# Doubling levels on half the columns, masks for four heads at once, and another place for GpSimd's selections

## What is computed

```python
# delta rule, per head and chunk: decay is exp of a difference of running sums, beta a gate
a = jnp.where(strict, jnp.einsum('nbhid,nbhjd->nbhij', k_beta, k) * decay, 0.0)
t_inv = lax.linalg.triangular_solve(a + eye, jnp.broadcast_to(eye, a.shape),
                                    left_side=True, lower=True, unit_diagonal=True)
u = t_inv @ (v * beta[..., None])
...
# choice of experts: 8 heads, the 16 best pairs out of 128 x 128 keys
sc = jnp.einsum("thpk,hpnk->thpn", q, sub_keys).astype(jnp.float32)
s_top, i_top = lax.top_k(sc, PEER_TOPK)
cand = s_top[:, :, 0, :, None] + s_top[:, :, 1, None, :]
cand_idx = i_top[:, :, 0, :, None] * PEER_NKEYS + i_top[:, :, 1, None, :]
best, pos = lax.top_k(cand.reshape(n_tok, PEER_HEADS, kk), PEER_TOPK)
idx = jnp.take_along_axis(cand_idx.reshape(n_tok, PEER_HEADS, kk), pos, axis=-1)
...
act = jax.nn.gelu(jnp.einsum("phkd,pd->phk", u_tab[idx], t))   # by experts, then summed with v_tab[idx]
```

## Time and profile before

| | |
|---|---|
| median of three runs | 2365.32 us |
| the profiled execution | 2366.43 us |
| its span on the core | 2364.6 us |
| mean granted TensorE clock | 0.958 of full speed |
| delta stage, first instruction to last | about 299.6 to 407 us of the span |
| choice of experts, the part with the 16 early tiles | about 1050 to 1179 us |
| TensorE busy | 91% of the span |
| GpSimd busy | 32% |

### The profile page before, as it was taken

One profiled execution on the slowest core, in us unless ns is written; L12 is line 12 of the kernel. 1 busy time (PEld: TensorE's weight loads), 2 busy tenths in 40 slices (PEclk: granted clock), 3 DMA queues, 4 the chain that ended last, 5 costly groups with the idle time before them and its releaser, 6 DMA issues. The chain is left out here.

```text
span 2364.6 us, 36245 instructions
## 1 busy us (share of the span) xinstructions
PE 2140.9 (91%) x11207; PEld 1878.7 (79%) x11207; DVE 1690.2 (71%) x3352; ACT 818.6 (35%) x1408; POOL 767.3 (32%) x677
## 2 busy tenths in 40 slices
PE   5998978569999987987699999999998999999997
PEld 4776777457777766867699999999996888888885
DVE  3576544548687664699377887887876888888886
ACT  4444322222322222323334444434432333333333
POOL 1000044000000000276467887887743222222220
PEclk9999999789999998998899999999999999999999
DMA  4432100132342504302277987887698999999995
GB/s 111 88 71 36 19 1 0 51 95 74 79 113 64 137 19 135 122 18 93 69 250 226 297 275 250 293 279 245 225 320 300 335 338 336 339 336 339 337 339 198
DMA packets 229948, 428.88 MB, mean 181 GB/s; under 512 B 18516, under 2 KB 155892, under 8 KB 229620
## 3 DMA queue, kind: packets, MB, share of 16 engines
q1 hardware_dynamic: 170976, 254.85, 34.9%
q0 software_dynamic: 41472, 151.01, 18.7%
q10 hardware_dynamic: 17428, 22.14, 2.6%
HBM read 381.80 MB, written 46.14 MB: 181 GB/s over the span
## 5 line engine op out<-in xcount | busy, mean ns | idle before, releaser
L1859 PE MATMUL bank<-xt_hi,u_hi 128*128 128x384 f32 x896 | 309.4, 345 | 0.0
L2139 PE MATMUL bank<-xt_hi 128*128 128x512 f32 x768 | 302.3, 394 | 7.5 <-DVE xt_lo L2068 7.5
L1859 PE MATMUL bank<-xt_hi,u_lo 128*128 128x384 f32 x896 | 300.5, 335 | 0.0
L1859 PE MATMUL bank<-xt_lo,u_hi 128*128 128x384 f32 x896 | 300.2, 335 | 0.0
L2139 PE MATMUL bank<-xt_lo,xt_hi 128*128 128x512 f32 x768 | 299.9, 390 | 0.0
L2139 PE MATMUL bank<-xt_hi,xt_lo 128*128 128x512 f32 x768 | 299.7, 390 | 0.0
L1721 POOL DMA_INDIRECT row_slot<-in_peer_v_dram,row_index x128 | 138.7, 1084 | 391.9 <-DVE row_x L2072 373.8
L2115 ACT ACTIVATE xt_hi<-xh 128x1024 fp32r<-128x1024 f32 x128 | 135.9, 1061 | 338.6 <-PE bank L2139 333.0
L2065 DVE TENSOR_TENSOR xt_lo<-xh,xt_hi 128x1024 fp32r<-128x1024 f32 x128 | 156.8, 1225 | 83.7 <-ACT xt_hi L2115 83.7
L1800 POOL TENSOR_TENSOR u_two<-u_match,u_weight_hi 128x512 fp32r<-128x512 f32 x96 | 180.3, 1878 | 96.9 <-DVE u_match L1886 96.4
L1392 POOL TENSOR_TENSOR k_wlo<-k_raw,k_whi 128x2048 fp32r<-128x2048 f32 x4 | 18.4, 4602 | 588.8 <-ACT k_whi L1511 588.8
(11 more groups left out here) (420 smaller groups left out, 4880.6 us busy)
## 6 DMA issues: line engine op xcount, KB each, us to landing
xh<-in_peer_v_dram SPq DMA_DIRECT2D x128, 512.0 KB, 5.4
xh<-in_peer_u_dram SPq DMA_DIRECT2D x113, 512.0 KB
x_raw<-in_w_in_dram SPq DMA_DIRECT2D x56, 512.0 KB, 5.4
v_ga<-acts SPq DMA_DIRECT2D x128, 192.0 KB
acts<-xh ACTq DMA_DIRECT2D x112, 192.0 KB
weights<-u_spread POOLq DMA_DIRECT2D x32, 512.0 KB
v_gg<-weights SPq DMA_DIRECT2D x128, 128.0 KB
p_raw<-in_w_in_dram SPq DMA_DIRECT2D x12, 1024.0 KB
```

Source lines behind the costliest of these rows:

```text
L1859: mm = pe.matmul(k.ps[4 + b][:, 0:DENSE], w[b][:, c, :], x[:, c, 0:DENSE], start=(c == 0 and w is uhi and x is hi), stop=(c == DC - 1 and ...
L2139: mm = pe.matmul(k.ps[q][:, :], h[b][:, t * P:(t + 1) * P], v[b][:, f], start=False, stop=False, skip_group_check=True)
```

## The change

In the delta stage the matmuls of levels 1 to 6 stream only the half of the columns that the level changes: 64 columns, taken in runs of 2^level elements out of `m`, `mt` or `x`, and written side by side into the first 64 columns of each head's part of the bank. The stationary operand stays 128 x 128. VectorE's subtractions and ScalarE's copies handle 128 x 256 elements, with the same runs on their SBUF side. `x` becomes one tile for each level, whose other half must be zero: GpSimd clears both chunks' tiles (128 x 3072 elements each) at the start of the stage, and ScalarE waits for that once. The inverse is written in two parts, the right half by VectorE, the left half by ScalarE, which copies it from `mt`; VectorE then waits for that copy (`inv_kept`) before it writes `mt` in the next turn. GpSimd's masks become one instruction of 128 x 512 for all four heads, 14 in a turn where 56 were.

In the choice of experts the list of GpSimd is: low 7, select(1, 0), low_early 0 and 1, select(1, 1), low_early 2 to 6, select(2, 0), low_early 7 and 8, select(2, 1), low_early 9 to 15.

```diff
--- before.py
+++ after.py
@@ -689,13 +689,32 @@
     heads = lambda ap: ap.rearrange("p (h n) -> p h n", h=H)
     with ExitStack() as st:
         two = lambda name: [k.sb(f"d_{name}{a}", [P, H, P], ctx=st) for a in range(2)]
-        qst, kst, vst, dec, at, m, mt, x, tmp = (two(n) for n in ("q", "k", "v", "dec", "at", "m", "mt", "x", "tmp"))
+        qst, kst, vst, dec, at, m, mt, tmp = (two(n) for n in ("q", "k", "v", "dec", "at", "m", "mt", "tmp"))
+        x = [k.sb(f"d_x{a}", [P, LEVELS - 1, H, P], ctx=st) for a in range(2)]
         ot = [k.sb(f"d_ot{a}", [P, LEVELS, H, P], ctx=st) for a in range(2)]
         small = [k.sb(f"d_small{a}", [P, 4, H], ctx=st) for a in range(2)]
         gb = two("gb")
+
+        def half(ap, lv, which):
+
+            return ap.rearrange("p h (b two s) -> p h b two s", two=2, s=2 ** lv)[:, :, :, which, :]
+
+        def half_of(ap, lv, which):
+
+            return ap.rearrange("p (b two s) -> p b two s", two=2, s=2 ** lv)[:, :, which, :]
+
+        def packed(bank, lv):
+
+            return bank[:, :, 0:P // 2].rearrange("p h (b s) -> p h b s", s=2 ** lv)
+
+        def packed_of(bank, h, lv):
+
+            return bank[:, h, 0:P // 2].rearrange("p (b s) -> p b s", s=2 ** lv)
+
+        x_zero = k.sem("d_x_zero")
         names = ("staged", "gc_ready", "gc_kept", "diff", "decay", "rates", "kk_ready", "qk_ready", "at_done", "intra_done",
                  "k_turned", "k_kept", "v_turned", "v_kept", "ot_done", "mt_done", "m_turned", "m_done", "x_ready",
-                 "x_kept", "dm_ready", "rate_diff")
+                 "x_kept", "dm_ready", "rate_diff", "inv_kept")
         s = {n: k.sems(f"d_{n}", 2) for n in names}
         last = LEVELS - 1
         k.credit()
@@ -741,6 +760,7 @@
 
                         dve.wait_ge(s["ot_done"][a], after(i * LEVELS + 1))
                         dve.wait_ge(s["dm_ready"][a], after(i * last))
+                        dve.wait_ge(s["inv_kept"][a], after(i))
                         for h in range(H):
                             dve.tensor_tensor(mt[a][:, h, :], k.ident[:, :], ot[a][:, 0, h, :], ALU.subtract
                                               ).then_inc(s["mt_done"][a], 1)
@@ -750,25 +770,28 @@
                             b1, b2 = heads(k.ps[4 * a + 1][:, :]), heads(k.ps[4 * a + 2][:, :])
                             dve.wait_ge(s["dm_ready"][a], after(i * last + lv))
                             if lv < last:
-                                dve.tensor_tensor(mt[a][:, :, :], mt[a][:, :, :], b2, ALU.subtract).then_inc(s["mt_done"][a], 1)
+                                rest = half(mt[a][:, :, :], lv, 1)
+                                dve.tensor_tensor(rest, rest, packed(b2, lv), ALU.subtract).then_inc(s["mt_done"][a], 1)
                                 dve.wait_ge(s["m_done"][a], after(i * last + lv))
-                                dve.tensor_tensor(m[a][:, :, :], m[a][:, :, :], b1, ALU.subtract).then_inc(s["m_done"][a], 1)
+                                part = half(m[a][:, :, :], lv, 0)
+                                dve.tensor_tensor(part, part, packed(b1, lv), ALU.subtract).then_inc(s["m_done"][a], 1)
                             else:
-                                dve.tensor_tensor(kept["inv"][:, c, :, :], mt[a][:, :, :], b2, ALU.subtract)
+                                dve.tensor_tensor(kept["inv"][:, c, :, P // 2:P], mt[a][:, :, P // 2:P], b2[:, :, 0:P // 2], ALU.subtract)
 
             MT = H + last - 1
 
             @block.gpsimd
             def _(pool):
+                for a in range(2):
+                    pool.memset(x[a][:, :, :, :], 0.0).then_inc(x_zero, 1)
                 with pool.Fori(0, TT // 2) as i:
                     for lv in range(LEVELS):
                         for a in range(2):
                             if lv == 0:
                                 pool.wait_ge(s["at_done"][a], after(i * H + H))
                                 pool.wait_ge(s["dm_ready"][a], after(i * last))
-                            for h in range(H):
-                                ins = pool.tensor_tensor(ot[a][:, lv, h, :], at[a][:, h, :], k.level[:, lv, :], ALU.mult)
-                            ins.then_inc(s["ot_done"][a], 1)
+                            pool.tensor_tensor(ot[a][:, lv, :, :], at[a][:, :, :], k.level[:, lv, :].unsqueeze(1).to_broadcast([P, H, P]),
+                                               ALU.mult).then_inc(s["ot_done"][a], 1)
 
             @block.scalar
             def _(act):
@@ -798,8 +821,14 @@
                         act.activation(m[a][:, :, :], heads(k.ps[4 * a][:, :]), ACT.Copy).then_inc(s["m_done"][a], 1)
                     for lv in range(1, LEVELS):
                         for a in range(2):
+                            c = i * 2 + a
+                            act.wait_ge(x_zero, after(a + 1))
                             act.wait_ge(s["x_ready"][a], after(i * last + lv))
-                            act.activation(x[a][:, :, :], heads(k.ps[4 * a][:, :]), ACT.Copy).then_inc(s["x_kept"][a], 1)
+                            act.activation(half(x[a][:, lv - 1, :, :], lv, 0), packed(heads(k.ps[4 * a][:, :]), lv), ACT.Copy
+                                           ).then_inc(s["x_kept"][a], 1)
+                            if lv == last:
+                                act.wait_ge(s["mt_done"][a], after(i * MT + MT))
+                                act.activation(kept["inv"][:, c, :, 0:P // 2], mt[a][:, :, 0:P // 2], ACT.Copy).then_inc(s["inv_kept"][a], 1)
 
             @block.tensor
             def _(pe):
@@ -845,7 +874,7 @@
                             pe.wait_ge(s["m_done"][a], after(i * last + lv))
                             pe.wait_ge(s["ot_done"][a], after(i * LEVELS + lv + 1))
                             for h in range(H):
-                                mm = pe.matmul(b0[:, h, :], ot[a][:, lv, h, :], m[a][:, h, :], start=True, stop=True)
+                                mm = pe.matmul(packed_of(b0, h, lv), ot[a][:, lv, h, :], half_of(m[a][:, h, :], lv, 0), start=True, stop=True)
                             mm.then_inc(s["x_ready"][a], 1)
                         for a in range(2):
                             b1, b2 = (heads(k.ps[4 * a + n][:, :]) for n in (1, 2))
@@ -856,8 +885,8 @@
                                 pe.wait_ge(s["intra_done"][a], after(i + 1))
                             for h in range(H):
                                 if lv < last:
-                                    pe.matmul(b1[:, h, :], mt[a][:, h, :], x[a][:, h, :], start=True, stop=True)
-                                mm = pe.matmul(b2[:, h, :], x[a][:, h, :], mt[a][:, h, :], start=True, stop=True)
+                                    pe.matmul(packed_of(b1, h, lv), mt[a][:, h, :], half_of(x[a][:, lv - 1, h, :], lv, 0), start=True, stop=True)
+                                mm = pe.matmul(packed_of(b2, h, lv), x[a][:, lv - 1, h, :], half_of(mt[a][:, h, :], lv, 1), start=True, stop=True)
                             mm.then_inc(s["dm_ready"][a], 1)
 
 
@@ -1581,19 +1610,22 @@
                 select(0, 0)
                 select(0, 1)
                 low(pool, 7)
-                select(1, 0)
-                select(1, 1)
 
                 def low_early(e):
                     pool.wait_ge(u_copied, after(4 * (e + 1)))
                     pool.tensor_tensor(u_lo[e % 4], u_turn[e % 2], u_hi[e % 4].bitcast(F32), ALU.subtract).then_inc(u_low, 1)
-                for e in range(5):
+                select(1, 0)
+                for e in range(2):
+                    low_early(e)
+                select(1, 1)
+                for e in range(2, 7):
                     low_early(e)
                 select(2, 0)
-                for e in range(5, EARLY - 1):
+                for e in range(7, 9):
                     low_early(e)
                 select(2, 1)
-                low_early(EARLY - 1)
+                for e in range(9, EARLY):
+                    low_early(e)
 
             @block.vector
             def _(dve):
```

## The result

The changed kernel takes 2408.77 us, the median of four runs (2408.09 to 2412.2), where the kernel before took 2366.06 beside it: a ratio of 1.0182, interval 1.0164 to 1.0199. I had forecast 2351.5, faster, in a range of 2336 to 2363.

What follows compares the result with a forecast made beforehand. TensorE's issue was taken to bound the delta levels, GpSimd the choice of experts. Levels -9.3, masks +11.2, clearing +5.3 and selections -21.2 took 2366.43 to 2352.4, forecast as 2351.5 us; own range 2345 to 2359, 8 in 10 2336 to 2363.

Steps and rivals of the forecast that it cites:

- every level at full clock (5.35 us): Delta stage: a level falls from 6.11 to 5.35 us, 0.76 less; 9.3 us gained in both turns.
- rival (4): Delta-stage levels: lighter stream lets TensorE's clock fall to 1.2 GHz, a level over 10 us, +48 in all: 2400; chance 0.11.
- Record, 0.104 us: TensorE in the delta levels: a 64-column record costs 0.104 us instead of 0.112.
- only the VectorE gap is won: Delta levels: bound if TensorE reads two-element runs at the old pace; the gain is then 5.9 us instead of 9.3.
- VectorE's half, 0.455 us: Delta levels: a 128 x 256 subtraction of a bank on VectorE takes 0.455 us instead of 0.69.
- ScalarE's added copy: Last delta level: copying the inverse's left half takes some 0.45 us and costs nothing; 0.2 us if it didn't fit.
- Masks, +5.6 a turn: Delta level 0: each VectorE subtraction waits for one whole four-head GpSimd mask of 1.15 us; +5.6 us a turn, +11.2 in all.
- Clearing, +5.3: Start of the delta stage: VectorE's copies go one for one with GpSimd's clearings of x, so the stage starts 5.3 us later.
- Selections, -21.2: Choice of experts: GpSimd's new order ends the stage 21.2 us sooner than the present 1178.65; bounds 17 and 24.
- late next, the exponentials: End of the experts' stage: ScalarE's exponentials, standing behind GELU 14, come next late, taking some 2 us with their table load.

Runs made afterwards that it cites:

- the fillers: The changed kernel plus eight matmuls of 512 columns a turn, results unread, on TensorE during the wait for `mt`: 2356.62 us, ratio 0.9952.
- level 1 whole: The changed kernel with level 1's matmuls streaming all 128 columns, levels 2 to 6 still 64: 2361.78 us, ratio 0.9972.
- the full stream with small masks: The changed kernel with all matmuls of the levels streaming 128 columns and one mask instruction for each head, clearing kept: 2340.78 us, ratio 0.9892.
- VectorE's halves alone: The kernel before with GpSimd's new selection order and VectorE subtracting only the half a level changes; 128 columns, no clearing: 2341.86 us, ratio 0.9903.
- the list alone: The kernel before with only GpSimd's new order in the choice of experts: 2344.54 us, ratio 0.9903.

## Why the prediction was wrong, point by point

- **The step that failed is the clock: the sum took every level at full clock (5.35 us) and put nothing in for a lower one.** That stood only in rival (4), to which I gave 0.11, and 2400; 2408.77 came. The size was right: "a level over 10 us", measured 10.23. The chance was wrong, and so was the question. I asked whether the new stream would let a high clock fall, and it doesn't (1.00 to the end of the levels with the fillers, and with level 1 whole). I should have asked at which clock the levels are entered. The answer stood in rows I had: the second window of rows 11, at 0.65, is the entry of the second turn, and the four transposes of rows 4 took 1.12 us, where they take 0.66 at full clock. The kernel before came in low in both turns and paid little for it: its first level took 6.38 and 6.81 us instead of 6.11, because with 128 columns the clock rose within level 1. With 64 it doesn't.
- **The two losses met this.** I had priced the longer wait for `mt` at its own length and not as a longer idle of TensorE. But it wasn't needed: with short masks (3.51 us) one turn still came in low.
- **Record, 0.104 us.** Wrong: I spread the 0.06 us between two groups of eight over their records. But both groups are seven steps of 0.111 us and the length of the last record, and only that differs (0.22 and 0.28 us, worked out from 1.00 and 1.06). From start to start it is 0.111 us, as with 128. At full clock the level is 5.53 us instead of the forecast 5.35; over ten levels this is 1.8 us of missing gain. It was the bound that I named ("only the VectorE gap is won", 5.9 us), and I should have taken it.
- **VectorE's half, 0.455 us.** Right: 0.42 with runs of two elements and more. ScalarE's added copy cost nothing that shows.
- **Masks, +5.6 a turn.** Right in its mechanism, measured +6.35; a mask takes 1.26 us and not 1.15. That VectorE instructions with two SBUF operands wait for a whole GpSimd instruction each, as the Trainium skill says (SBUF: State Buffer, Who interferes with whom), is borne out: 9.87 us for eight beside masks of 1.26 us, against 3.51 with short masks.
- **Clearing, +5.3.** Right: TensorE's first block starts 4.7 us later after VectorE's first copy, and level 1, less the masks, 5.7; two copies each last about as long as one clearing (2.61 and 2.95 us beside 2.66 and 2.94). The trace with the eight fillers has one copy of 5.20 us behind both clearings instead, with the same wait of TensorE. Moved, the clearing gives back 5.6 us up to level 1 in the trace, and 3.6 in the median of the runs.
- **Selections, -21.2.** Right to the tenth in the trace, and 2344.54 us alone. What I named as late next, the exponentials, is what VectorE waits for. The tenth is luck: the steps on the way lie up to some 2 us off (select(2, 0) takes 9.6 us and not 11.5).
- So at full clock the change takes 2356.62 us (with fillers), 5 us above the forecast and inside its range. What was taken for a small chance outweighed four terms of the right size and one that was 1.8 us off.

**Open.** What decides at which clock a turn comes in. Here are the second transposes of the first turn in two kernels with 128 columns, short masks and the same wait, first the full stream with small masks, then VectorE's halves alone:

```profile
320.93 0.66 PE L870 MATMUL bank<-ident,d_mt 128*128 128x128 f32 x4 [1.19 <-DVE d_mt L765]
```

```profile
314.04 1.12 PE L847 MATMUL bank<-ident,d_mt 128*128 128x128 f32 x4 [1.19 <-DVE d_mt L750]
```

The first kernel comes in high in both turns; the second in both low, as do the kernel before and the list alone. With short masks and 64 columns the two turns differ. In the first turn, where nothing before the levels differs but the clearing, the two kernels with the early clearing came in high, and the three without it came in low; that is all these traces show, and no run tells which earlier work counts.

## What to carry to other kernels

Before a stream of matmuls is made lighter, read the granted clock in the windows just ahead of it: if it is low there and the heavy stream is what raises it, the lighter one can stay at half speed to its end, and one heavier level (or fillers in the wait) at the entry was enough here. Take the price of a record from start to start, never from a group's length. When one instruction is made of four, ask who waits for it: here each of VectorE's subtractions waited for one whole mask, 1.26 us where it had been 0.42.

## What the runs showed of the hardware

- The clock has two stable answers to the same work. With 64-column fp32 records, TensorE busy without a gap: 30 records in 6 us at 0.50 for six levels, or 55 in 6 us at 1.00 for six levels, by the clock at the entry. With 16 of 48 records at 128 columns, or one whole level of them, the first turned into the second inside level 1.
- At full clock an fp32 record with its own 128 x 128 weights comes every 0.111 us, with 64 columns as with 128; at 1.2 GHz it comes every 0.21 us, again with both (sixteen records of ot x m in 3.62 us). The Trainium skill (TensorE: Matmul & The Clock Gate, Back-to-back issue gap) gives about 60 cycles for up to 64 columns. At 2.4 GHz 0.111 us are some 267 cycles, so no run here comes near it. Each record here has a weight load of its own; whether that is the reason, no run separates.
- A VectorE copy from SBUF of 0.43 us lasts 2.61 and 2.95 us beside clearings of 2.66 and 2.94 us, though a clearing reads nothing.
